# An attention stage in which the value products, the gate tiles and six convolution taps change places

## The reference, cut to what matters

```
def stick_breaking_attention(q, k, v):          # 8 heads, HEAD_DIM 64, query blocks of 128
    for start in range(0, s_len, Q_BLOCK):
        z = jnp.einsum("bqhd,bkhd->bhqk", qf[:, start:end], kf[:, :end])
        log_keep = jnp.where(causal, jax.nn.log_sigmoid(-z), 0.0)
        log_after = lax.cumsum(log_keep, axis=3, reverse=True) - log_keep
        a = jnp.where(causal, jnp.exp(jax.nn.log_sigmoid(z) + log_after), 0.0)
        outs.append(jnp.einsum("bhqk,bkhd->bqhd", a, vf[:, :end]))

def hybrid_mixer(...):
    u = u_val * jax.nn.sigmoid(u_gate)
    u = causal_depthwise_conv(u, conv_w, conv_b)               # 31 taps
    u = jax.nn.silu(layernorm(u, conv_ln_g, conv_ln_b))
    y_conv = u @ w_conv_out
    y_att = o.reshape(b, s, ATT_WIDTH) @ w_att_out
    merged = jax.nn.sigmoid(g_conv) * y_conv + jax.nn.sigmoid(g_att) * y_att
    return merged @ w_o
```

## Time and profile before

| what | value |
|---|---|
| median of 3 executions | 1336.4 us (1336.11 to 1338.03) |
| the profiled execution | 1336.14 us, of which the span is 1334.3 us |
| PE busy | 1314.1 us, 98% of the span |
| DVE busy | 983.0 us, 74% |
| ACT busy | 553.2 us, 41% |
| DMA | 141 GB/s mean |
| granted clock of PE | 0.998 of 2.4 GHz |
| chain of work that ended last | PE 84%, DVE 8%, ACT 3%, DMA 3%, issue 2% |

### The profile page before, as it was taken

How to read it: one execution, slowest core, us unless ns; L and a number is a source line. 1 busy time by engine, 2 the same in 40 slices (tenths; PEclk the granted TensorE clock), 3 DMA queues, 4 the chain that set the end, 5 groups by cost and what they waited for, 6 DMA issues and landing times.

```text
span 1334.3 us, 15752 instructions
## 1 busy us (share of the span) xinstructions
PE 1314.1 (98%) x6395; PEld 1065.0 (80%) x6395; DVE 983.0 (74%) x1218; ACT 553.2 (41%) x767; POOL 87.9 (7%) x153
## 2 busy tenths in 40 slices
PE   7999999999999999999999999999999999999997
PEld 4799688778888888888788777778878888888886
DVE  4787877989778777777759799866795444446988
ACT  4553444344333333232332566774443222224543
POOL 0000000000001000100000011000002120000001
PEclk9999999999999999999999999999999999999999
DMA  9543056325455556654232211122204333225565
GB/s 391 195 136 133 4 170 207 125 81 187 158 173 176 183 162 206 221 203 163 87 106 95 88 65 46 56 95 95 95 32 156 115 116 105 98 103 199 192 221 195
DMA packets 34472, 188.01 MB, mean 141 GB/s; under 512 B 4304, under 2 KB 5088, under 8 KB 18016
## 3 DMA queue, kind: packets, MB, share of 16 engines
q1 hardware_dynamic: 20976, 140.32, 29.7%
q0 software_dynamic: 13424, 46.69, 11.0%
HBM read 182.79 MB, written 4.20 MB: 140 GB/s over the span
## 4 chain that ended last, share of the span: by engine, by line
PE 84%; DVE 8%; ACT 3%; DMA 3%; issue 2%; SPq 0%; DVEq 0%; ACTq 0%
PE bank L1678 25%; PE bank L1680 24%; PE bank L1679 24%; PE bank L2017 2%; PE bank L2018 2%; PE bank L2023 2%; DVE WL L938 2%; DMA raw<-weights 1%; PE bank L1883 1%; DMA adaf<-ada 1%; DVE ada_acc L980 1%; PE bank L2213 1%; ACT WH L448 1%; PE bank L2183 1%; PE bank L2201 1%
## 5 line engine op out<-in xcount | busy, mean ns | idle before, releaser
L1678 PE MATMUL bank<-hH,WH 128*128 128x512 f32 x992 | 390.1, 393 | 0.8 <-DVE WL L938 0.5
L1680 PE MATMUL bank<-hH,WL 128*128 128x512 f32 x992 | 386.4, 390 | 0.0
L1679 PE MATMUL bank<-hL,WH 128*128 128x512 f32 x992 | 386.2, 389 | 0.0
L938 DVE TENSOR_TENSOR WL<-raw,WH 128x2048 fp32r<-128x2048 f32 (+1 forms) x114 | 253.5, 2226 | 153.9 <-ACT WH L448 153.9
L448 ACT ACTIVATE WH<-raw 128x2048 fp32r<-128x2048 f32 (+1 forms) x117 | 218.0, 1865 | 237.4 <-DMA raw<-weights 180.0
L1678 PEld LDWEIGHTS bank<-hH,WH 128*128 128x128 f32 x992 | 186.3, 188 | 42.6 <-issue 3.3
L1680 PEld LDWEIGHTS bank<-hH,WL 128*128 128x128 f32 x992 | 186.2, 188 | 39.2
L1679 PEld LDWEIGHTS bank<-hL,WH 128*128 128x128 f32 x992 | 186.4, 188 | 37.7 <-issue 0.2
L980 DVE SCALAR_TENSOR_TENSOR ada_acc<-ada_half,csil,ada_acc 128x1024 f32<-128x1024 f32 x70 | 89.6, 1280 | 5.6 <-DMA ada_half<-ada_later 3.0
L1427 DVE SCALAR_TENSOR_TENSOR cacc<-uT,vec,cacc 128x511 f32<-128x511 f32 (+29 forms) x120 | 83.2, 753 | 0.0
L401 POOL DMA_DIRECT2D ada_half<-ada_later x80 | 42.4, 530 | 570.7 <-DVE ada_acc L980 335.1
(11 more groups left out here) (358 smaller groups left out, 2147.3 us busy)
## 6 DMA issues: line engine op xcount, KB each, us to landing
raw<-weights SPq DMA_DIRECT2D x119, 1024.0 KB, 5.0
ada_half<-ada_later POOLq DMA_DIRECT2D x80, 512.0 KB, 4.5
adaf<-ada SPq DMA_DIRECT2D x8, 1024.0 KB, 19.9
xT<-x_t SPq DMA_DIRECT2D x4, 512.0 KB, 5.8
x_rows<-xB POOLq DMA_DIRECT2D x32, 64.0 KB, 2.2
gF<-x_rows POOLq DMA_DIRECT2D x3, 512.0 KB, 6.9
ctxT<-ctx_t SPq DMA_DIRECT2D x1, 1024.0 KB, 28.3
out_t<-gF SPq DMA_DIRECT2D x2, 512.0 KB, 2.6
```

Source lines behind the costliest of these rows:

```text
L938: TT_(lo_of(c, 0, width), raw_of(c, 0, width), hi_of(c, 0, width), sub).then_inc(s.lo_done, 1)
L1678: mm(o, lh, rh, start=start, stop=False, skip_group_check=skip)
L1679: mm(o, lh, rl, start=False, stop=False, skip_group_check=skip)
L1680: return mm(o, ll, rh, start=False, stop=stop, skip_group_check=skip)
```

## The change

On PE, in a round with two gate halves, the order was values(j-1), scores(j+1), half, arguments(j), half; it becomes scores(j+1), half, values(j-1), arguments(j), half. In a short round it was values(j-1), scores(j+1), half, arguments(j); it becomes scores(j+1), values(j-1), arguments(j), half. In round 16, which has no scores and no arguments, values(15) stood ahead of the last half and now stands behind it. On ACT the copy of gate tile 5 moves from round 5 to round 6. On DVE six taps leave the rounds 3, 6, 7, 8, 10 and 11 and go to the key stage (two), the value stage (two) and the query stage (two).

```
-TAPS_AT = (2, 7, 4, 10, 5, 5, 7, 8, 5, 5, 7, 6)
+TAPS_AT = (2, 7, 4, 9, 5, 5, 6, 7, 4, 5, 6, 5)
...
-                if 7 <= j <= 10:
+                if 6 <= j <= 10:
                     gate_copy(j - 1)
...
-                if 0 <= j <= 5:
+                if 0 <= j <= 4:
                     gate_copy(j)
...
+                    if i == 3 and c0 == C_V2 or i == 1 and c0 == C_Q2:
+                        conv_taps(2)
                     dve.wait_ge(ready, done(C_V2 + 1, i, 4) if c0 == C_V2 else i + 1)
...
                     ins.then_inc(s.bank_free, 1)
+                    if c0 == C_K2 and n:
+                        conv_taps(1)
...
+                if j + 1 < PAIRS:
+                    scores(j + 1)
+                if j == PAIRS or j >= 0 and HALVES[j + 1] == 2:
+                    gate_half()
                 if j >= 1:
                     values(j - 1)
-                if j + 1 < PAIRS:
-                    scores(j + 1)
-                if j >= 0:
-                    gate_half()
                 if 0 <= j < PAIRS:
                     arguments(j)
-                    if HALVES[j + 1] == 2:
-                        gate_half()
+                    gate_half()
```

## The result

The changed kernel takes 1339.56 us in the median of 13 runs, the kernel before 1336.7 in 13 runs beside them: 2.9 us more. The ratio is 1.0021, with a 95% interval of 1.0014 to 1.0029: longer for certain, by an amount that lies around the 0.2% at which the prediction drew its border. The profiled execution took 1338.79 us with a span of 1337.0, where that of before took 1336.14 with 1334.3: 2.7 us more.

A forecast was written before the change was run, and what follows sets the result against it. PE's own instruction list was taken to bound the attention. Terms 2.4 - 0.8 + 1.6 - 0.4 = +2.8 us on the profiled 1336.14, adjusted for the median and rounding, gave 1339.1 us; range 1336.3 to 1340.8.

The forecast's parts named there:

- The seams of the full rounds: PE, attention rounds: four changes of product shape instead of three, about 0.2 us each round; +2.4 us for twelve rounds.
- The stalls behind the short rounds: PE, values(5) and values(10): 1.2 us of stall goes, rounds 6 and 11 pay +0.4 for seams; net -0.8 us.
- The end of the stage: Attention to merge: values(15) now last, so the merge's first product waits for DVE's head_pair(3); +1.57 us, summed as 1.6.
- Given back in the merge: Merge, third and fourth rounds: PE's waits for DVE's sums vanish because the weight-chunk chain gets more lead; -0.4 us.
- The taps: DVE: six taps of 0.75 us moved to the key to query stages, hidden in both places; nothing.
- Rival 1: PE, values to arguments: weight loads pulled ahead make that seam free; -1.3 us in all, 1335.1, chance 13%.
- Rival 2: PE, arguments(5) and (10), a half earlier, wait for low parts; whole cover lost once +2.7 us, 1341.8; chance 13%.
- Rival 3: Attention to merge: DVE's two instructions are overlapped, so the end costs only the seam; +1.2 us, 1337.6, chance 7%.
- rival 4: PE, short rounds: values(5) and values(10) still wait; +1.2 us, 1340.3, chance 5%.

The follow-up runs named there:

- the last round undone: Changed kernel with values(15) ahead of the last gate half again in round 16; median 1338.35 us, ratio 1.0014 to the kernel before.
- the late copy: Changed kernel, but values ahead of scores in all rounds and, in round 10, ACT's gate copy behind the exponential; 1335.35 us, ratio 0.9990 to before.
- the last round alone: Kernel before with only values(15) moved behind the last gate half; median 1337.31 us, ratio 1.0004.
- the full-array run: Changed kernel with every values product over all 128 array columns, sums not those of the task; executed once for its trace, attention 139.87 us.
- the last version: The late copy with ACT making the merge's next weight-chunk high part ahead of the gate sigmoids; median 1336.11 us, ratio 0.9999 to before.

## Why the prediction was right

The forecast was 1339.1 us, from a sum of 2.8 us over the kernel before; 1339.56 was measured, 2.9 over the kernel before beside it, and 2.65 between the two profiled executions. Going through its terms:

- *The seams of the full rounds.* Right in kind: scores and values each have their own entry of 0.09, and the unseen seam, values to arguments, costs as much as values to a gate half. The sum charged 0.2 us in each of fourteen rounds, 2.8 us in all. Two runs that differ in just this, the last round undone (134.87) and the late copy (132.34, without waits), are 2.53 us apart, 0.18 a round. From arguments(0) to arguments(11) alone, where no end of the stage can matter, they are 1.92 us apart over eleven rounds, 0.17 each. So the term was 0.3 too large; rounding 0.19 up to 0.2 makes 0.14 of that, the rest I can't assign.
- *The stalls behind the short rounds.* 1.2 us predicted; 133.49 - 132.34 = 1.15 measured, when they are taken away without the seams. Right. The change as made removes them too, since scores and another half come in between; with the old order of values and scores 0.44 us of them stay, which the prediction did not see since it asked only how long the exponential takes, not what stands ahead of it in ACT's list.
- *The end of the stage.* 1.6 predicted; 1.56 and 1.52 by the two runs, with a wait of 1.64 in the trace. Right.
- *Given back in the merge.* 0.4 predicted, 0.22 in the trace. The mechanism is right in the main: the third round's wait is gone and the fourth's is smaller. But the sum let all waits go, and the fourth round was to begin after 0.23 us; 0.14 us stayed there, and 0.08 came in at the merge's first product. Nor did the lead last: against the merge's first product ACT starts on the third chunk 2.76 us behind instead of 4.99, on the next one 15.99 instead of 16.26, since it then waits 0.30 us for a transfer. The size varies from run to run: without the lead of the late merge its length was 44.04 to 44.80 us in six kernels with the old end and the merge's old order, with it 43.82 to 43.96 in four. The trace of before, the shortest of the six, could not tell that the payback is between 0.1 and 1.0 us.
- *The taps.* Nothing predicted, nothing measured, in both directions.

The measured terms give 2.53 - 1.15 + 1.56 - 0.22 = 2.72, but that they add up to the difference of the spans is no proof: the first three come from a chain of traces from before over the late copy and the last round undone to after, and must close. Not forced by that chain are the 1.92 us over eleven rounds, the row by row seams, and the 1.52 us of the last round alone. That the total was met to 0.1 us is in part luck: the seams were put 0.27 too high, and the payback 0.18 too high with the other sign.

Rival 1, the free fourth change, is refuted by the row at 763.52 and by the full-array run. The Trainium skill, in "TensorE: Matmul & The Clock Gate", "Step-by-step: what each phase is for", says that weight loads are pulled ahead of running products when the row groups don't conflict or the background buffer is the target. In these traces loads run ahead between neighbours of one shape (762.74 in the full-array run), and not across a change of it (0.17 us of idle loader ahead of 763.52). The Trainium skill, in "TensorEngine Tiling (Array Packing)", Key Properties, says that a change of the tiling mode drains TensorE; the idle loader agrees with that.

Rival 2, a wait for the low parts, did not occur: 2.15 us of lead, 1.9 predicted. Rival 3, a hidden end, is refuted by PE's wait of 1.64 us, and rival 4, stalls that stay, by the 0.58 and 0.80 us of values(5) and values(10).

The chances were near even between no change and slower because the sum lay on the border of 0.2%. The measured ratio lies there too, 1.0021 with 1.0014 to 1.0029 around it: that the kernel became slower is sure, on which side of the border it is the runs do not say.

## What to carry to other kernels

When an engine is full, read its cost from the distance of starts, and list the seams between unlike products: a reordering that separates two odd-shaped groups standing side by side adds a seam per round, and here fourteen of them (2.5 us) outweighed two removed stalls (1.15 us). Do the local repair instead of the general one: moving only what stalled, and one copy on the engine that feeds it, took 1.15 us out of the stage, about 0.1% of the whole. And look at what the moved work used to cover at the end of the loop; the last filler ahead of a hand-over between engines is worth as much as the hand-over takes (1.6 us), less what the later start gives back behind it (0.1 to 1.0 us here).

## What the runs showed of the hardware that I had not expected

- Two float32 products over all 128 columns of the array, one behind the other, took 0.50 us to the second product behind them for 128 columns each, and two over 64 columns each took 0.53, side by side. For 128 columns, packing the two heads won nothing; its gain comes with width: 1.78 us against 1.17 by the same measure for 512 columns in round 4.
- The weight load behind a group of another shape starts only when that group is nearly through. In the rows read here it came 0.07 to 0.08 us ahead of the modelled end of the group: scores and values behind a gate product (759.28 against 758.97 + 0.39, 763.15 against 762.83 + 0.39), arguments behind values (763.52 against 763.15 + 0.44), and before the change scores and a gate product behind values. Between neighbours of one shape, in the full-array run, the load started with the gate product ahead of it, 0.39 us ahead of that product's end.
- Two executions can differ by several microseconds before the stage in question begins. The profiled run of the last version was 1340.07 us long, while that kernel's fastest was 1333.61. Its granted clock was 1.00 until 20 us, 0.50 from 22 to 30, and 1.00 again from 32 us on; PE had waited 1.41 us for a transfer at 18.67. At PE's same instructions it lay 0.97 us behind the changed kernel ahead of this stretch (20.25 against 19.28) and 4.92 behind it (33.16 against 28.24), and in between its gate products came 0.43 us apart instead of 0.23; so the low clock took most of these 4 us. The clock is not all of it: the run of the late copy, with 1.00 throughout, had scores(0) 2.1 us late.
